# Recurrence stage: a tile's key transpose, state product and two halves of its values a half-level apart, and the gate's Silu with a first square root ahead of round two

## What is computed

```python
def _hgrn2_chunk(S0, xs):
    q, k, v, g = xs
    G = jnp.cumsum(g, axis=1)
    decay = jnp.exp(jnp.where(causal, G[:, :, None] - G[:, None, :], -jnp.inf))
    att = jnp.einsum('bthk,btshk,bshk->bhts', q, decay, k)
    o = (jnp.einsum('bhts,bshv->bthv', att, v)
         + jnp.einsum('bthk,bhkv->bthv', q * jnp.exp(G), S0))
    S = (jnp.exp(G_end)[..., None] * S0
         + jnp.einsum('bshk,bshv->bhkv', k * jnp.exp(G_end[:, None] - G), v))
# then, for all tokens:
    ob = ob * lax.rsqrt(jnp.mean(ob * ob, axis=-1, keepdims=True) + EPS)
    ob = ob.reshape(B, T, B_VW) * g_norm * jax.nn.silu(gb)
```

## Time and profile before

| what | us |
|---|---|
| median of 3 runs | 2988.79 |
| lowest, highest | 2984.78, 2991.47 |
| the profiled execution | 2991.18 |
| its span in the trace | 2989.3 |
| recurrence stage in it, from barrier to barrier | about 120 (728.9 to 848.7) |

### The profile page before, as it was taken

One profiled execution on the slowest core, in us unless ns is written; L12 is line 12 of the kernel. 1 busy time (PEld: TensorE's weight loads), 2 busy tenths in 40 slices (PEclk: granted clock), 3 DMA queues, 4 the chain that ended last, 5 costly groups with the idle time before them and its releaser, 6 DMA issues. The chain is left out here.

```text
span 2989.3 us, 61068 instructions
## 1 busy us (share of the span) xinstructions
PE 2854.5 (95%) x24985; PEld 2653.3 (89%) x24985; DVE 1742.2 (58%) x3136; ACT 1006.3 (34%) x2102; POOL 1533.6 (51%) x1377
## 2 busy tenths in 40 slices
PE   6999999997789999999999999999999999999998
PEld 4859999765689999999999999956699999999998
DVE  6399999656646744434787500066648543446785
ACT  3351111355433433333232311156525333333232
POOL 2121224464523777776577232144424777776675
PEclk8999999998889999999999999999999999999999
DMA  6716763652341122124222223163121212224321
GB/s 220 246 69 227 252 222 122 175 180 64 103 170 57 51 86 86 65 86 145 86 86 86 77 91 114 43 219 113 65 90 51 84 68 87 78 74 137 123 69 69
DMA packets 192053, 338.85 MB, mean 113 GB/s; under 512 B 27784, under 2 KB 107424, under 8 KB 189920
## 3 DMA queue, kind: packets, MB, share of 16 engines
q1 hardware_dynamic: 138832, 266.50, 26.7%
q10 hardware_dynamic: 52944, 68.45, 6.6%
HBM read 268.30 MB, written 79.49 MB: 116 GB/s over the span
## 5 line engine op out<-in xcount | busy, mean ns | idle before, releaser
L109 PE MATMUL tr_acc<-tr_quad_hi,ah_ring_hi 128*128 128x264 f32 x2432 | 694.1, 285 | 7.7 <-ACT tr_kept L1160 2.5
L740 POOL TENSOR_TENSOR ah_ring_lo<-ah_raw,ah_ring_hi 128x512 fp32r<-128x512 f32 (+2 forms) x426 | 578.9, 1366 | 237.6 <-ACT ah_ring_hi L1149 147.0
L111 PE MATMUL tr_acc<-tr_quad_hi,ah_ring_lo 128*128 128x264 f32 x2432 | 692.7, 285 | 0.0
L110 PE MATMUL tr_acc<-tr_quad_lo,ah_ring_hi 128*128 128x264 f32 x2432 | 690.3, 284 | 0.0
L109 PEld LDWEIGHTS tr_acc<-tr_quad_hi,ah_ring_hi 128*128 128x128 f32 x2432 | 458.7, 189 | 9.4 <-ACT tr_kept L1160 3.0
L110 PEld LDWEIGHTS tr_acc<-tr_quad_lo,ah_ring_hi 128*128 128x128 f32 x2432 | 458.7, 189 | 0.1
L111 PEld LDWEIGHTS tr_acc<-tr_quad_hi,ah_ring_lo 128*128 128x128 f32 x2432 | 458.2, 188 | 0.0
L2917 DVE CUSTOM_DVE_ANT_0 pc_prob<-pc_dots,pc_bias 128x640 f32<-128x640 f32 (+4 forms) x128 | 79.0, 655 | 283.1 <-POOL pc_bias L2720 261.7
L1779 DVE TENSOR_SCALAR_CACHE_REDUCE f_q<-score,choose_trial 128x384 bf16<-128x384 f32 (+6 forms) x224 | 242.2, 1145 | 1.1
L2083 POOL CAST f_w_hi<-f_raw 128x512 fp32r<-128x512 f32 x66 | 46.7, 708 | 375.9 <-DMA f_raw<-in_w_dram 204.8
L738 POOL CAST ah_ring_hi<-ah_raw 128x512 fp32r<-128x512 f32 (+1 forms) x114 | 72.6, 637 | 283.7 <-PE tr_acc L111 263.0
(11 more groups left out here) (410 smaller groups left out, 7448.4 us busy)
## 6 DMA issues: line engine op xcount, KB each, us to landing
f_ada_w<-in_w_ada_dram SPq DMA_DIRECT2D x48, 1024.0 KB, 5.7
scratch_inner<-tr_kept ACTq DMA_DIRECT2D x88, 264.0 KB, 2.3
ah_raw<-in_w_gate_dram SPq DMA_DIRECT2D x44, 512.0 KB, 3.5
ah_raw<-in_w_up_dram SPq DMA_DIRECT2D x44, 512.0 KB, 4.5
ah_raw<-in_w_down_dram SPq DMA_DIRECT2D x64, 256.0 KB, 3.0
f_raw<-in_w_dram SPq DMA_DIRECT2D x24, 512.0 KB, 7.9
out_z_dram<-f_stage ACTq DMA_DIRECT2D x60, 176.0 KB, 2.0
out_z_dram<-tr_value ACTq DMA_DIRECT2D x48, 176.0 KB, 1.9
```

The source lines that it names most:

```text
L109: pe.matmul(out, w_hi, hi, start=start, stop=False, skip_group_check=onto)
L110: pe.matmul(out, w_hi, lo, start=False, stop=False, skip_group_check=onto)
L111: return pe.matmul(out, w_lo, hi, start=False, stop=stop, skip_group_check=onto)
L740: pool.tensor_tensor(lo[:, 0:width], own, hi[:, 0:width].bitcast(F32), ALU.subtract).then_inc(w_ready, 1)
```

## The change

Steps of a tile move in the lists:

| step | engine | offset before | offset after |
|---|---|---|---|
| `turn_keys`, `turned_keys` | PE, ACT | 0 | -1; for a round's first tile ahead of the round |
| `updates` | PE | 1 | 0 |
| `values`, heads 0 and 1 | PE | 1 | 1 |
| `values`, heads 2 and 3 | PE | 1 | 2 |
| `state_update` | DVE | 2 | 3 |
| `squares` | ACT | 3 | 3 |
| `inverse_roots` | DVE | 4 | 5 |
| `scaled` | ACT | 5 | 5 |
| `turn_out` | PE | 6 | 6 |
| `finish` | DVE | 7 | 6 |

`LAST`, the number of half-levels of a round, goes from 16 to 15. The gate's Silu moves on ACT from behind the first `turned_keys` to ahead of it, right behind round one's `place`, and a square root of the one-column tile `eps` follows it there. This puts the table load of the square root at that place and not at the first `squares`. Core of the diff:

```diff
-    LAST = 2 * LEVELS + 2
+    LAST = 2 * LEVELS + 1
...
-                    for t in tiles_at(n - 1, at, 2):
+                    for t in tiles_at(n - 1, at, 3):
                         state_update(t)
-                    for t in tiles_at(n - 1, at, 4):
+                    for t in tiles_at(n - 1, at, 5):
                         inverse_roots(t)
-                    for t in tiles_at(n - 1, at, 7):
+                    for t in tiles_at(n - 1, at, 6):
                         finish(t)
...
+            def gate_silus():
+                act.wait_ge(own.gate_in, 16)
+                act.activation(gate[:], gate[:], ACT.Silu).then_inc(gate_silu, 1)
+                act.wait_ge(eps_set, 1)
+                act.activation(root_first[:], eps[:], ACT.Sqrt)
...
-                    for t in tiles_at(n - 1, at, 0):
-                        turned_keys(t)
+                    if at >= 3:
+                        for t in tiles_at(n - 1, at, -1):
+                            turned_keys(t)
...
                 place(n)
+                if n == 0:
+                    gate_silus()
+                if n + 1 < ROUNDS:
+                    turned_keys(3 * n)
...
             for n in range(ROUNDS):
+                if n:
+                    turn_keys(3 * (n - 1))
                 for pr in range(2):
                     pairs(n, 0, pr)
...
+                    if at >= 3:
+                        for t in tiles_at(n - 1, at, -1):
+                            turn_keys(t)
                     for t in tiles_at(n - 1, at, 0):
-                        turn_keys(t)
+                        updates(t)
                     for t in tiles_at(n - 1, at, 1):
-                        updates(t)
-                        values(t)
+                        values(t, first_heads)
+                    for t in tiles_at(n - 1, at, 2):
+                        values(t, last_heads)
```

More of the change, by code:

```diff
@@ L3275, in recurrence @@
         eps = m.sb("hg_eps", [P, 1])
+        root_first = m.sb("hg_root_first", [P, 1])
         ring = [[m.ps(f"hg_ring{b}{pr}", [P, 512]) for pr in range(2)] for b in range(2)]
@@ L3537, in _ @@
                 silus(n)
+            def gate_silus():
[3 more added lines that the diff above has]
+                act.activation(root_first[:], eps[:], ACT.Sqrt)
             def gate_scale(hd):
[L3540 to L3543, removed]
+                act.wait_ge(gate_silu, 1)
                 act.activation(gate[:, hd, :], gate[:, hd, :], ACT.Copy, scale=head.gnorm[:, hd:hd + 1]).then_inc(gate_done, 1)
             act.wait_ge(att_zero, 2)
-            act.wait_ge(eps_set, 1)
             def place(n):
@@ L3680, in updates, with values @@
                 last.then_inc(dS_done, 1)
-            def values(p):
+            def values(p, heads):
                 t = tile_at[p]
@@ L3702, in values @@
                 bank_free(pe, "out", p)
-                for hd in range(HB):
+                for hd in heads:
                     own_out = bank("out", p)[:, P * hd:P * hd + P]
@@ L3706, in values @@
                     last = pe.matmul(own_out, r[:, hd, P * t:P * t + P], state[s][:, hd, :], start=False, stop=True)
-                last.then_inc(out_done, 1)
+                if heads[-1] == HB - 1:
+                    last.then_inc(out_done, 1)
             def turn_out(p):
@@ L3714, in turn_out @@
                 last.then_inc(o_turned, 1)
+            first_heads, last_heads = range(HB // 2), range(HB // 2, HB)
             for n in range(ROUNDS):
+                if n:
+                    turn_keys(3 * (n - 1))
                 for pr in range(2):
@@ L3732, in _ @@
             updates(TILES - 2)
-            values(TILES - 2)
+            values(TILES - 2, range(HB))
             updates(TILES - 1)
-            values(TILES - 1)
+            values(TILES - 1, range(HB))
             turn_keys(TILES)
             updates(TILES)
-            values(TILES)
+            values(TILES, range(HB))
             turn_out(TILES - 2)
```

## The result

The changed kernel takes 3008.8 us in the median (3005.05 to 3012.92 over 6 runs), the kernel before 2988.12 us (2983.05 to 2991.47). The ratio is 1.0073, with a 95% interval of 1.0063 to 1.0083: **slower by 20.7 us** between the medians. The forecast was 2999.8 us with a range of 2988 to 3006 us. The direction was right, the forecast change was about half of what came, and the time lies above the range.

A forecast was written before the change was run, and what follows sets the result against it. Waits between engines in the recurrence stage were taken as the bound: +5.1 us at full clock, plus 1.9 and 4 us for PE's lower clock, gave +11 us on 2988.8, so 2999.8 us, range 2988 to 3006 us.

The forecast's parts named there:

- the chain of waits: Recurrence stage: waits between engines, not any engine's sum of work, set the time; +5.1 us at full clock.
- the gate: Head of round two: keys' copy queues behind the Silu's late load, so half-level 2 comes 3.2 to 5.1 us later.
- the first stretch of round two: PE from half-level 2 to 6: 9.4 us instead of 11.59, a gain of 2.2 us.
- the middle stretch: PE from half-level 6 to 10: 10.0 us instead of 8.47 and 8.29, so +1.5 and +1.7 us.
- the term for the clock: PE at half clock around idle gaps: 1.9 us at the head plus 4 of 7.2 us for the other six.
- the upper bound: Whole stage, lower clock in every idle stretch: +14.2 us, against +5.1 us at full clock.
- the first stretch of round three: PE from half-level 2 to 6: 9.4 us instead of 10.60, a gain of 1.2 us.
- the head of round three: Last turn_out of round two to round three's half-level 2: 0.9 us less than 7.72, half the values leaving it.
- the ends: Half-level 10 to a round's last turn_out: 7.3 us instead of 5.82 and 5.81, +1.5 us twice.
- the first: Rival: PE's clock holds at full nearly throughout the stage; +3 to +7 us, 2994 us; chance 0.20.
- the stalls balance (2): Rival: head no worse, middle stretches' losses cancel first stretches' gains; about 2989 us, within 3 us; chance 0.15.
- rival 3: Halved values fill PE's waits, stretches shrink toward PE's own work; -7 us, 2982 us; chance 0.05.

The follow-up runs named there:

- e1: Changed kernel with the gate's part undone (keys' copy ahead of the Silu again, small root left out): 3008.26 us, ratio 1.0069.
- e9: The same kernel as e1, profiled and timed once more: 3008.52 us, ratio 1.0061.
- e4: Changed kernel with 58 unused filler products in PE's waits: 3005.67 us, ratio 1.0055.
- e3: Changed kernel with both DVE offsets undone (state update at 2, reciprocal at 4): 2991.68 us, ratio 1.0018.
- e2: Kernel before with only the gate's part of the change (Silu and first root ahead of the keys' copy): 2989.48 us, ratio 1.0005.
- e7: Changed kernel with both DVE offsets and the gate's part undone; PE's order and finish at 6 stay: 2986.09 us, ratio 0.9997.
- e8: Changed kernel with state update at 2, reciprocal at 3, squares ahead of next keys' copy, first keys ahead of Silu, gate scalings moved: 2977.59 us, ratio 0.9956.
- e12: The same as e8 with the Silu and first root ahead of the first keys' copy again: 2985.25 us, ratio 0.9987.
- e10: The same kernel as e4, profiled and timed once more: 2999.55 us, ratio 1.0036.

## Why the prediction was right or wrong

**Right: the chain of waits.** The loss is in the stage. The waits named were found with about their sizes: the gate's landing and the 4.4 us of the late copy, the wait of 0.89 us for the state update (about 1.0 forecast), that of 2.27 us for the scaled output (2.3), the gain in the first stretch of round two (9.45 us, and 9.4 was worked out). At full clock the chain is right: from `turn_out` to `turn_out` the middle stretch takes 9.75 us (e1), and 10.0 us was worked out from mark to mark.

**Wrong: the term for the clock.** I priced a stretch at half clock at 1.3 us, from the one such case of values, and then took a little over half of the 7.2 us. Measured are 2.05 us in a middle stretch (11.8 against 9.75), since the lower clock covers halves of the values on both sides of the wait, and in round two `turn_out` as well. Both middle stretches of the changed kernel's profile had it, and neither first stretch (1.00 and 0.97), though all four end in a wait of 2.27 us. So the share was wrong too: from 765 to 785 us the granted clock was 0.91, where I had named a value below 0.8 as a sign of being right. Even the upper bound, +14.2 us, was built from the too small price: the stage grew by 19.9 us. The rule of the Trainium skill that the prediction cites from "TensorE: Matmul & The Clock Gate", section "HAM oscillation — how this bites in real kernels", would have given 3003 us and so was nearer than my middle value. But the trace does not show each step at the low clock, and of the four middle stretches of e1 and e9, with the same waits, three kept a clock of 1.00.

**Half right: the first stretch of round three.** It came at +0.2 and looks like the value at half clock (+0.1). It is not: the clock was 0.97, and PE stood still for 0.82 and 0.56 us without a wait that the profile shows. The 10.60 us of before, which I took as the chain's own, held such waits too, of 1.13 and 0.20 us, and a part at half clock (granted 0.84):

```profile
799.96 0.85 PE L3646 MATMUL hg_ring<-hg_r,hg_k 128*32 128x32 f32 x72 [1.13 <-issue]
```

So the gain of 1.2 us in the sum was no gain of the new order alone.

**Wrong: the head of round three.** I gave it -0.9 us and no share of the clock at all. It came at +1.8: from 796.41 to 806.00 all of PE's work there ran at half clock (granted 0.51 over 796.4 to 806.0), the state product in 2.08 us and not in 1.16, half of the values in 1.83. PE had stood still for 3.73 us ahead of it, for the scaled output, where it was 1.42 before. That is 2.7 us missing from the sum; 0.4 of them is a longer wait without a cause in the profile (0.64 against 0.20 us).

**Wrong: the ends.** I took `rise` at 0.55 us. In the end of round two three of them met POOL and took 3.5 us, 1.9 us more than three alone. e4 has the clock at 1.00 there and still takes 7.50 us between the last two `turn_out` rows of round two, as the changed kernel does with 7.49, so in this place it is DVE beside POOL and not PE's clock. e3 takes 5.09 us there. In round three they took 2.2 us, and the clock is about half of the excess: from the mark to `turn_out` 2.65 us, against 1.49 in e1 at full clock. Missing from the sum: about 1.6 and 1.2 us over the upper bound.

**Half right: the gate.** Its head cost is there in the trace, 4.75 us to the first mark. Its worth in time depends on what else is late: 0.05% alone on the old order (e2), 0.04 to 0.12% on the changed one (e1, e9), 0.21% with DVE's steps back (e3 against e7), 0.31% in the best version (e8 against e12). Only the last is clear of the intervals. I added it as a fixed 3.2 to 5.1 us. Adding it to the others was wrong by up to its whole size.

**The rivals.** The clock doesn't hold, so the first falls. That the stalls balance (2) and that the halves fill the gaps (3) fall too. What rival 3 described does exist: e8 keeps the halves and reaches PE's own work in the middle stretch. Its condition was the right one, that state update and reciprocal are off the chain, and the change moved them the other way.

**What stays open.** The "issue" waits of PE sum to between 3.4 and 12.0 us of a stage in the profiles, and to 3.4 and 8.8 in two of the same kernel (e10, e4). What causes them no run tells. Because of them and the clock, one profile's stage length is uncertain by several us. The medians of e1 and e9, which don't show the 4 us that the head can gain, are explained only in part: e9's profile shows an execution in which such waits ate the gain, and no run tells how often that happens. What decides in which stretch the clock falls is open too.

## What to carry to other kernels

In a chain through several engines, a step that is moved one place back in its engine's list waits for all that the place ahead of it waits for: look at what the instruction in front needs, and whether the waiter's own earlier work is part of it. Here two DVE steps of 0.2 and 1.1 us, moved behind one `rise`, made 16 us out of six tiles, the lower clock that came with the gaps included. A load's landing time decides where its first use may stand on an engine, and nothing urgent belongs behind it. When PE gets new gaps of 2 to 3 us in each step, price the work on both sides of the gap at half clock as one end of the range: of the six middle stretches of the changed kernel, e1 and e9, three had it.

## What the runs showed of the hardware

- Filling PE's waits with 48 to 58 useless products held the granted clock at 1.00 in the middle stretches and made the kernel faster by 5 to 13 us: on the changed kernel in two measurements (the smaller gain, e4's, is within the intervals), on e1 in one. The same stretch took 11.8 us at 0.80 and 9.62 us filled.
- With equal instructions the clock falls in one execution and not in another: e1's and e9's middle stretches took 9.75, 9.75, 9.76 and 11.67 us. Within one execution it falls in one step and not in the next: 1.00 in the changed kernel's first stretch of round two, 0.80 in the second, behind equal waits.
- PE stood still for up to 3.67 us at once (e3; 3.39 in e2 and e9) without a wait that the profile shows.
- A DVE product of two SBUF tiles of 128x384 took 0.54 to 0.56 us alone or when it began 0.04 us ahead of POOL's product, and up to 1.4 us when it began behind it (1.20 at 790.17 and 1.37 at 733.11 in the changed kernel). One that reads PSUM was not slowed (1.11 and 1.12 us for four).
- A table load took 1.28 us, with the next instruction 0.01 to 0.02 us behind it, in both places of the stage in every profile.
